# Mixture-of-experts stage of a two-block network: token and hidden transposes moved from TensorE to VectorE blocks, rows moved through DRAM

## The reference, cut to what matters

```python
def _moe_swiglu(h, router, w_gate, w_up, w_down):
    logits = (xt @ router).astype(jnp.float32)            # xt: 256 x 1024
    top_logit, top_e = lax.top_k(logits, TOP_K)           # 2 of 8 experts
    gates = jax.nn.softmax(top_logit, axis=-1)
    ...
    # per block of tokens of one expert e:
    #   (silu(x @ w_gate[e]) * (x @ w_up[e])) @ w_down[e]
    y = jnp.zeros_like(xt).at[s_tok].add(yb[dest] * s_gate[:, None])

xl = xl + g2 * _moe_swiglu(hl, ...)                       # g2: one gain per feature
return _rmsnorm(xl, final_g)
```

## Time and profile before

| | us |
|---|---|
| median of 3 runs | 2807.41 |
| lowest, highest | 2804.67, 2808.72 |
| span of the profiled execution, first to last instruction | 2797.1 |

### The profile page before, as it was taken

One profiled execution on the slowest core, in us unless ns is written; L12 is line 12 of the kernel. 1 busy time (PEld: TensorE's weight loads), 2 busy tenths in 40 slices (PEclk: granted clock), 3 DMA queues, 4 the chain that ended last, 5 costly groups with the idle time before them and its releaser, 6 DMA issues. The chain is left out here.

```text
span 2797.1 us, 55858 instructions
## 1 busy us (share of the span) xinstructions
PE 2678.6 (96%) x24711; PEld 1724.3 (62%) x24711; DVE 1118.0 (40%) x2214; ACT 440.6 (16%) x1021; POOL 209.6 (7%) x229
## 2 busy tenths in 40 slices
PE   8999999999989899999999888899999999999998
PEld 6668988844568588884774577735344353544535
DVE  3477375246764468767434665500000000000001
ACT  1311101014332120000023242300000000000001
POOL 0000000000124001111000034000000000000000
PEclk9999999999999999999999999899999999999999
DMA  7365475421300124436532300499999999999995
GB/s 257 106 240 181 151 271 187 149 75 60 114 2 3 61 76 159 147 100 223 188 113 90 84 32 3 160 320 395 334 402 362 344 393 349 386 342 390 376 339 199
DMA packets 182657, 570.89 MB, mean 204 GB/s; under 512 B 24816, under 2 KB 37228, under 8 KB 166042
## 3 DMA queue, kind: packets, MB, share of 16 engines
q1 hardware_dynamic: 159731, 505.70, 50.0%
q0 software_dynamic: 13856, 53.11, 5.4%
q10 hardware_dynamic: 8839, 8.59, 1.0%
HBM read 566.15 MB, written 1.23 MB: 203 GB/s over the span
## 5 line engine op out<-in xcount | busy, mean ns | idle before, releaser
L1260 PE MATMUL bank<-normed,weight_ring 128*128 128x256 f32 (+2 forms) x1760 | 360.6, 365 | 15.6 <-DVE normed L1146 8.6
L3157 PE MATMUL bank<-work 128*32 128x384 f32 (+1 forms) x3840 | 360.0, 529 | 0.0
L1260 PEld LDWEIGHTS bank<-normed,weight_ring 128*128 128x128 f32 x1760 | 307.6, 191 | 66.2 <-issue 19.4
L1260 PE MATMUL bank<-work,weight_ring 128*128 128x256 f32 (+2 forms) x1104 | 283.6, 417 | 4.3 <-PEq L2775 2.2
L713 PE MATMUL bank<-normed,weight_ring 128*128 128x512 f32 (+1 forms) x832 | 278.2, 494 | 0.0
L3157 PEld LDWEIGHTS bank<-work 128*32 128x32 f32 x3840 | 122.3, 110 | 222.3 <-issue 222.3
L1260 PEld LDWEIGHTS bank<-work,weight_ring 128*128 128x128 f32 x1104 | 209.4, 192 | 75.7 <-issue 52.6
L245 DVE SCALAR_TENSOR_TENSOR work<-work,small 128x512 f32<-128x512 f32 x336 | 239.6, 755 | 17.9 <-DMA work<-in_mod_w 11.2
L3157 PE MATMUL bank<-weight_ring,work 128*32 128x512 f32 (+1 forms) x2304 | 234.7, 561 | 10.0 <-issue 8.9
L713 PEld LDWEIGHTS bank<-normed,weight_ring 128*128 128x128 f32 x832 | 157.5, 190 | 118.5 <-issue 108.3
L3285 DVE TENSOR_TENSOR work<-bank,work 128x512 f32<-128x512 f32 (+1 forms) x48 | 27.0, 618 | 501.6 <-PE bank L3157 501.6
(11 more groups left out here) (380 smaller groups left out, 2742.2 us busy)
## 6 DMA issues: line engine op xcount, KB each, us to landing
work<-in_moe_w_down SPq DMA_DIRECT2D x64, 1024.0 KB, 12.6
work<-in_mod_w POOLq DMA_DIRECT2D x48, 1024.0 KB, 5.6
work<-in_moe_w_gate SPq DMA_DIRECT2D x64, 768.0 KB, 5.2
weight_ring<-in_w_in SPq DMA_DIRECT2D x40, 1024.0 KB, 5.1
weight_ring<-in_moe_w_gate SPq DMA_DIRECT2D x32, 1024.0 KB, 15.3
work<-in_moe_w_gate SPq DMA_DIRECT2D x32, 1024.0 KB, 14.0
work<-in_moe_w_up SPq DMA_DIRECT2D x32, 1024.0 KB, 11.4
weight_ring<-in_moe_w_up SPq DMA_DIRECT2D x32, 1024.0 KB, 6.7
```

The lines of the kernel that those rows point to most:

```text
L1260: last = nc.tensor.matmul(self.banks(gi)[j][:, to], w[:, k, j * P:(j + 1) * P], a, start=k0 + k == 0, stop=k0 + k == final)
L3157: last = nc.tensor.matmul(self.bank[3 * up + a][g * R:(g + 1) * R, 0:n], xg[place_of(x)][:, k, a * R:(a + 1) * R], w[:, g * n:(g + 1) * n] ...
```

## The change

What is done in the items is laid out anew:

- The moving operand of gate and up takes strided columns: group g reads, in every 128 columns, the 32 from g x 32 on, instead of one quarter of the tile in one piece. The hidden values of the four groups then are such that transposing each square of 32 x 32 by itself (VectorE's `transpose`) gives `hid` in the form that the down product wants. TensorE's `turn_hidden` and ScalarE's copies go.
- Tokens of an item come from DRAM. `x_dram` holds the normed tokens as four rows of 256 floats each, ordered so that a transposition of 32 x 32 squares gives `xg`. A table in DRAM (`table_dram`), cleared, filled by four indirect DMAs and read back, says which token is in which slot; GpSimd gathers 3 x 128 rows of 1 KB per item by indirect DMA, one item ahead. Only the first item's tokens still come by the 0/1 product.
- Outputs of all items but the last are multiplied by the gain row on VectorE, stored to `y_dram` by four DMAs on ScalarE's queue, and recalled by four indirect DMAs (4 x 128 rows of 4 KB) during the last item, where VectorE adds them with the gate values into `z`, the residual by token rows. Before, `y_dram` (12 x 96 rows of 4 KB, 4.7 MB) is filled with zeros by one DMA on SyncE's queue, behind the first twelve weight tiles. Only the last item's outputs go through `spread` and a sum on TensorE.
- The down product writes banks 6 and 7 (`out_of`).
- The final norm works on `z` by token rows; no transposes back.
- Routing and items are one block. Six items are written out, then the loop, then the last item with its own code. Semaphores are taken over from earlier stages (`renamed`).

The core of the diff (a `-` line is of before, a `+` line of after):

```diff
-FIXED_ITEMS = N_EXPERTS - 1
+FIXED_ITEMS = N_EXPERTS - 2
+        def out_of(a):
+            return self.bank[6 + a // 2][:, (a % 2) * quarter:(a % 2 + 1) * quarter]
 # SyncE
+                sync.wait_ge(constants.sem, constants.at(1))
+                sync.dma_start(bass.AP(y_dram, 0, [[A * quarter, P], [ITEM_TOKENS * D, I - 1], [1, A * quarter]]),
+                               xr.rearrange("p a c -> p (a c)").unsqueeze(1).to_broadcast([P, I - 1, A * quarter])).then_inc(blanked.sem, 16)
 # GpSimd
+                pool.dma_start(table_rows, blank[0:R]).then_inc(cleared.sem, 16)
+                for t in range(2):
+                    pool.wait_ge(rowsm.sem, rowsm.at(t + 1))
+                    nc.gpsimd.tensor_copy(quartered[:, t]..., xtok[:, t]...).then_inc(constants.sem, 1)
+                    pool.dma_start(x_dram.ap()[4 * t * P:4 * (t + 1) * P, :]..., quartered[:, t]).then_inc(xstored.sem, 16)
+                pool.wait_ge(spotted.sem, spotted.at(1))
+                for i in range(4):
+                    pool.indirect_dma_start(out=table_dram.ap(), out_offset=..., in_=token_i[:, i // 2:i // 2 + 1]...).then_inc(listed.sem, 16)
+                pool.wait_ge(listed.sem, listed.at(64))
+                for g in range(4):
+                    pool.dma_start(table_i[g * R:(g + 1) * R].bitcast(F32), table_rows).then_inc(tabled.sem, 16)
+                def gather_next(named):
+                    pool.wait_ge(asked.sem, named)
+                    for a in range(A):
+                        pool.indirect_dma_start(out=xr[:, a], in_=x_dram.ap(), in_offset=...next_i[:, a:a + 1]...).then_inc(landed.sem, 16)
 # TensorE, routing: turn(xT, 0), turn(xT, 1) and the gate row are new
+                turn(hT, 0, (4, 5)).then_inc(rows.sem, 1)
+                norm.add_up(pe, self.bank[3])
+                score(0)
+                pe.wait_ge(rowsm.sem, rowsm.at(1))
+                turn(xT, 0, (4, 5)).then_inc(xturned.sem, 1)
+                score(1)
+                turn(hT, 1, (6, 7)).then_inc(rows.sem, 1)
 ...
+                turn(xT, 1, (4, 5)).then_inc(xturned.sem, 1)
+                for g in range(4):
+                    for h in range(2):
+                        last = nc.tensor.matmul(self.bank[3][g * R:(g + 1) * R, h * P:(h + 1) * P], gate_column(2 * g + h).to_broadcast([P, R]), ident,
+                                                start=True, stop=True)
 # TensorE, item
-                                    last = nc.tensor.matmul(self.bank[3 * up + a][g * R:(g + 1) * R, 0:n], xg[place_of(x)][:, k, a * R:(a + 1) * R], w[:, g * n:(g + 1) * n],
-                            if part == 0 and k == 1:
-                                scatter()
-                            if part == 2 and k in (3, 4, 5):
-                                turn_hidden(0, k - 3)
+                            w = full_tile(part * DT + k)[:, 0:4 * n].rearrange("p (b g j) -> p g b j", g=4, j=R)
+                                    last = nc.tensor.matmul(self.bank[3 * up + a][g * R:(g + 1) * R, 0:n].rearrange("p (b j) -> p b j", j=R), xg[:, a, k], w[:, g],
+                    pe.wait_ge(flipped.sem, x * (2 * A) + flipped.at(A))
 # ScalarE, item
+                    act.wait_ge(ymoved.sem, x * A + ymoved.at(A))
+                    for g in range(4):
+                        act.dma_start(to[:, :, g * quarter:(g + 1) * quarter], y[g * R:(g + 1) * R]).then_inc(ystored.sem, 16)
 # VectorE, item
+                        for a in range(A):
+                            dve.wait_ge(mult.sem, x * (2 * A) + mult.at(A * s + a + 1))
+                            nc.vector.transpose(to, hk[:, s, a, 0:n]).then_inc(flipped.sem, 1)
+                        dve.wait_ge(landed.sem, x * (16 * A) + landed.at(16 * A))
+                        nc.vector.transpose(xg.rearrange("p a f r -> p (a f r)"), xr.rearrange("p a c -> p (a c)")).then_inc(xready.sem, 1)
+                    dve.wait_ge(used.sem, x * per + used.at(per))
+                        dve.wait_ge(ystored.sem, x * 64 + ystored.at(0))
+                    for a in range(A):
+                        nc.vector.tensor_tensor(y[:, a], out_of(a), gate_row, ALU.mult).then_inc(ymoved.sem, 1)
```

## The result

The median of four runs is 2714.65 us (2712.74 to 2718.04), against 2806.04 for the kernel before on the same chip (2801.78 to 2808.72): a ratio of 0.9675, 95% interval 0.9663 to 0.9687, 91.4 us less. The direction and the mechanism were right; the size was not.

The account below looks back on a forecast made before the run. TensorE's own queue was taken as the bound, weights hidden with little to spare. Terms -85.2 + 3.2 + 1.3 - 0.6 + 15 = -66.3 us gave span 2730.8, plus 10.3: 2741 us, range 2716 to 2790.

Parts of the forecast that it names:

- leaves TensorE: In the items: removed transposes, scatters, token gathers and the hole at seven boundaries take 85.2 us off TensorE's chain.
- routing: Before the items: added transposes and gate products on TensorE, less a block boundary, net +3.2 us (bounds 0 and 6).
- loops: One more item in the counted loop and item-count reads in mid-stage: +1.3 us (between 0 and 2.6).
- tail: After the items: VectorE products replace ScalarE's y copies and transposes back go, about -0.6 us (bounds -2 and +2).
- waits for the stream: In the items: TensorE waits for weights as the twelve-slot ring's lead shrinks, 768 KB tiles at 375 GB/s: +15 us.
- The check in the prediction: Items of 966 us less 85 leave 881, or 110 per item; the products alone were put at 109 us.
- Moves to VectorE: Block transposes and y products, together about 5 us per item; VectorE busy near 11 us per item, taken as costing nothing.
- The time around the span: Whole execution: the median of the runs lies 10.3 us above the profiled span, and this difference was kept.
- A: Rival, chance 0.25: in the items the stream hides after all, total change -81.3 us, 2726 us.
- B: Rival, chance 0.25: in the items the stream becomes the bound, 116 us per item, +47 us on 2726, 2773 us.
- C: Rival, chance 0.10: strided moving weights slow the gate and up products by 20%, +116 us, 2842 us.
- D: Rival, chance 0.05: in the items a new wait, table landing or recall, replaces the old ones; 2800 us if 60 us long.

Follow-up runs that it names:

- the strided run: The kernel before with only the moving weights of gate and up read in runs of 32, all else kept: 2804.18 us, ratio 0.9999.

## Why the prediction was wrong in size

Stage against stage it is -88.6 us measured and -66.3 predicted. By the prediction's own steps:

| step | predicted | measured | from |
|---|---|---|---|
| leaves TensorE | -85.2 | -97.6 | 966.1 to 868.5, the items without waits |
| routing | +3.2 | -0.6 | 25.1 to 24.5 |
| loops | +1.3 | 0 | no gap between items |
| tail | -0.6 | -1.6 | 14.0 to 12.4 |
| waits for the stream | +15 | +11.1 | 868.5 to 879.6 |

**What leaves TensorE** is the step that failed: a term of the sum that was too small by 12.4 us. Each link of the chain was counted by the time it occupies, and a link's removal frees more. About 10.3 us (8 x 1.3) lie in the products around the removed pieces: an item of before, without its pieces and its hole, takes 117.63 - 1.10 - 2.80 - 3.21 - 0.81 = 109.7, and the same products alone take 108.42. The two kernels with added transposes show 0.14 us per visit for this, or 1.1 per item, and the 0.2 behind each hole is the rest. The gathers, five more visits, bring 0.7 (the items with one gather pair take 123.17, 5.54 more than their neighbours, for a link of 5.40). Another 1.7 are the first 48 products, which ran at the low clock before: 7.05 us against 5.36 in the later items. From these 12.7 goes 0.3, since the `gated` transposes that stay in the last item cost 1.13 us there (109.55 - 108.42) and the prediction had left them 0.81. That makes the 12.4. The check in the prediction had the warning in it: 110 us per item by the links, 109 by the products. That 1 us in each of eight items was passed over, and the 109 was still too high: its links of products, 13.09 us for 240 for one, hold the same 0.14 and 0.2. Rates from start to start of uninterrupted groups (96 products of 512 in 10.30 us at 1932.53) make it 108.4.

**Routing** had the added work right: with the clock late it is 27.4, +2.3 on before, near the +3.2. With the clock early it is 24.5. The profiled execution was of the early kind, and the prediction had priced the gather at the low clock.

**The stream** was named with its place (part 0 and the first tiles, landing over 15 us, above 400 GB/s) and nearly its size. The mechanism, a lead of twelve slots that shrinks from item to item, is shown: zeros cut, -6.6 us; small rows gone, no wait left. The rate assumed for 768 KB tiles, 375 GB/s, was too low: from 1970 to 1990 of after, where the weights that move are all of such tiles, the window has 415, and 44.04 + 0.79 MB in 108.4 us are 413. With 415 in place of 375 the prediction's own sum is 40.4 + 30.3 + 35.8 + 1.9 + 0.5 = 108.9 us. Against the items of 110 us that I expected, that would have left next to no waits; they came because TensorE needs only 108.4. Two errors of the prediction met here. The Trainium skill, page "HBM Reference", section "Specifications (TRN2)", has about 425 GB/s for a core that streams alone; the window of after's routing shown above has 426, its items 407.

**Moves to VectorE** came out as said: 72.17 / 8 = 9.0 us per item ("near 11"), never the releaser. The block transposes lie at or inside their bounds: 547 ns, just under the 551 of the product, and 936 under the 1300.

**The time around the span.** I kept 10.3 us between the span and the median of before. The runs show 1.8 to 2.2 us between an execution's span and its own time; the rest was a profiled execution some 8 us faster than the median, and its untouched part is 7.6 us shorter than that of after. Taking -66.3 from the median directly gives the same 2741, so this didn't cause the error, but it hid how far the untouched part moves. Of the 26.4 us between forecast and result, 22.4 lie in the stage, 1.4 in the median of before (2806.04 beside after, 2807.41 earlier), and the rest, under 3, is what one execution differs from the medians.

**The rivals.** A came nearest in time (2726) and is refuted in kind: the stream doesn't hide. B's mechanism is real but not its price: the DMA share is 1.00 and yet the waits are 11 us and not 47. That the result lies nearer to A than to the forecast is luck for A: its waits of 0 were wrong by 11.1 us, and the term that all of them shared by 12.4 the other way. C falls with the strided run. D did not happen; the table's landing kept VectorE 16.3 us and the zeros' landing GpSimd 14.2 us in the first item, both off the path.

## What to carry to other kernels

Small work of another shape between the products of a full TensorE costs more than its own rows: price its removal from the rate of an uninterrupted group of products, not by adding up links. When TensorE gets faster, set the stream's bytes against the new time: once the DMA share is 1.00, a MB moved anywhere ahead (here cleared rows that nobody needed cleared) can come back as a wait hundreds of us later (6.6 us for 2.75 MB in one comparison, 3.0 in the other), and placing it elsewhere helps little. Compare two executions by stages from a common point, since the untouched part varied by 8 us here.

## What the hardware showed beyond that

- A change from products with 32-wide stationary operands to full transposes and back costs 0.29 us per visit beside the transposes themselves, 0.14 of it in no row of its own.
- VectorE's transposition of 32 x 32 squares in float32 takes as long as a product of the same width: 681 against 684 ns for 512 columns, 547 against 551 for 384.
- TensorE's clock stayed at 1.2 GHz for 17 us in one execution of after (from 1802.4 to 1819.5, by its granted clock in steps of 1 us) and for 24 in another (1798.8 to 1822.7), with the same instructions in routing.
- Weights, 1 KB rows and the cleared rows together moved at 407 to 412 GB/s over some 870 us, at a DMA share of 1.00 to 1.02; from 1970 to 1990, where the weights were 768 KB tiles alone, at 415.
